# Delta-rule branch: decay columns of all heads made ahead of head 0, the rate moved into the exponent, pieces and queue positions changed

## What is computed

```python
g = jnp.cumsum(g, axis=-1)
decay = jnp.exp(jnp.where(incl, g[..., :, None] - g[..., None, :], -jnp.inf))
k_beta = k * beta[..., None]
a_mat = jnp.einsum("bhnid,bhnjd->bhnij", k_beta, k) * jnp.where(strict, decay, 0.0)
sol = lax.linalg.triangular_solve(eye + a_mat, rhs, left_side=True, lower=True, unit_diagonal=True)
qk = jnp.einsum("bhnid,bhnjd->bhnij", q, k) * decay
q_dec = q * jnp.exp(g)[..., None]
k_dec = k * jnp.exp(g_last - g)[..., None]
# scan over chunks
v_new = u_c - w_c @ s
o = qd_c @ s + qk_c @ v_new
s = s * jnp.exp(gl_c) + kd_c^T @ v_new
```

## Time and profile before

| | us |
|---|---|
| median of 3 runs | 3056.8 |
| lowest, highest | 3055.17, 3057.97 |
| profiled execution, its own time | 3061.32 |
| profiled execution, its span | 3059.6 |

### The profile page before, as it was taken

One profiled execution on the slowest core, in us unless ns is written; L12 is line 12 of the kernel. 1 busy time (PEld: TensorE's weight loads), 2 busy tenths in 40 slices (PEclk: granted clock), 3 DMA queues, 4 the chain that ended last, 5 costly groups with the idle time before them and its releaser, 6 DMA issues. The chain is left out here.

```text
span 3059.6 us, 38554 instructions
## 1 busy us (share of the span) xinstructions
PE 2888.3 (94%) x15219; PEld 2356.4 (77%) x15219; DVE 1299.4 (42%) x1953; ACT 1072.4 (35%) x1829; POOL 1206.5 (39%) x805
## 2 busy tenths in 40 slices
PE   6999999999999969578778999999999999999998
PEld 5878787877888846477667887878888888888887
DVE  5233233321479949666564353322233232232323
ACT  4241313243044539455544122332333333333232
POOL 2222122121123320423421433466666666766663
PEclk9999999999999979878798999999999999999999
DMA  4434233343545357210103546332322333332331
GB/s 114 165 132 140 80 102 102 100 132 94 184 148 176 120 189 249 80 44 31 73 31 126 179 141 208 105 100 93 102 91 91 103 96 124 97 97 91 114 110 58
DMA packets 239571, 352.78 MB, mean 115 GB/s; under 512 B 32928, under 2 KB 186272, under 8 KB 239392
## 3 DMA queue, kind: packets, MB, share of 16 engines
q1 hardware_dynamic: 239392, 350.32, 35.2%
HBM read 263.71 MB, written 96.36 MB: 118 GB/s over the span
## 5 line engine op out<-in xcount | busy, mean ns | idle before, releaser
L102 PE MATMUL pj_acc<-u_hi,pj_w_hi 128*128 128x512 f32 x1464 | 576.6, 394 | 10.6 <-DVE u_lo L823 10.6
L2763 DVE TENSOR_TENSOR x_tm<-m_ps,x_tm 128x512 f32<-128x512 f32 x384 | 265.0, 691 | 745.8 <-PE m_ps L104 745.8
L104 PE MATMUL pj_acc<-u_hi,pj_w_lo 128*128 128x512 f32 x1464 | 571.9, 391 | 0.0
L103 PE MATMUL pj_acc<-u_lo,pj_w_hi 128*128 128x512 f32 x1464 | 571.7, 391 | 0.0
L551 POOL TENSOR_TENSOR pj_w_lo<-pj_w_raw,pj_w_hi 128x1024 fp32r<-128x1024 f32 x61 | 159.2, 2610 | 722.0 <-ACT pj_w_hi L600 722.0
L2645 POOL TENSOR_TENSOR m_lo<-gate,held 128x1024 fp32r<-128x1024 f32 x96 | 237.8, 2500 | 270.0 <-ACT held L2562 270.0
L102 PEld LDWEIGHTS pj_acc<-u_hi,pj_w_hi 128*128 128x128 f32 x1464 | 275.9, 188 | 85.7 <-issue 18.2
L104 PEld LDWEIGHTS pj_acc<-u_hi,pj_w_lo 128*128 128x128 f32 x1464 | 276.1, 189 | 58.2
L103 PEld LDWEIGHTS pj_acc<-u_lo,pj_w_hi 128*128 128x128 f32 x1464 | 276.2, 189 | 56.2
L102 PE MATMUL m_ps<-held 128*128 128x512 f32 x768 | 299.7, 390 | 2.4 <-DVEq L2744 2.4
L102 PE MATMUL m_ps<-held,m_h_hi 128*128 128x512 f32 x768 | 299.5, 390 | 0.0
(11 more groups left out here) (308 smaller groups left out, 4939.8 us busy)
## 6 DMA issues: line engine op xcount, KB each, us to landing
gate<-in_w_mlp_dram SPq DMA_DIRECT2D x48, 1024.0 KB, 5.4
gate<-in_w_mlp_dram SPq DMA_DIRECT2D x96, 512.0 KB, 3.7
proj<-pj_stage SPq DMA_DIRECT2D x61, 768.0 KB, 3.4
pj_w_raw<-in_w_in_dram SPq DMA_DIRECT2D x61, 512.0 KB, 5.2
gate<-proj SPq DMA_DIRECT2D x24, 768.0 KB, 4.4
mo_w_raw<-in_w_out_dram SPq DMA_DIRECT2D x48, 256.0 KB, 2.9
rpb_bias<-pj_shut SPq DMA_DIRECT2D x48, 192.0 KB, 3.1
rpb_bias<-rpb_near SPq DMA_DIRECT2D x24, 384.0 KB
```

Of the source, the lines that this page charges most:

```text
L102: pe.matmul(out, w_hi, x_hi, start=first, stop=False)
L103: pe.matmul(out, w_hi, x_lo, start=False, stop=False)
L104: return pe.matmul(out, w_lo, x_hi, start=False, stop=last)
L2763: dve.tensor_tensor(xt, ps2[:, q % 4], xt, ALU.add).then_inc(added, 1)
```

## The change

- The columns of all 4 heads are made once: `gneg` (minus the cumulated decay), `gbeta` (decay plus the logarithm of beta, by ACT's Ln) at the head of attention, and `cx` in head 0's preparation. The chunks' last rows come from two matmuls of a broadcast column of the identity with `cols`; they stand in front of `gram(0, 0)` on PE and wait for two DVE copies, which stand behind DVE's wait for the norm weights' DMA. `decay_columns` and `columns` at k = 6 are gone.
- Beta enters the exponent, so `scores` is one instruction of 128x512.
- `decayed_queries` is 6 pieces of 128x512. The exponentials of `gq` move from k = 0 and 2 of the solve phase to steps 5 and 6 of the scan before (for head 0 into its preparation).
- ACT's `cut_blocks` moves ahead of the output copies of step 2, DVE's behind the state copies of step 2. Of the 16 placing copies into `un`, ACT now makes 4 (of `c1`, after the first transpose), DVE 12.
- The positions in the solve phase and in the scan move as the constants say. `out_lengths` is split into 3 pieces of 8 matmuls at k = 3, 4, 5. `out_gate` goes from k = 12 to k = 15, the sigmoid product (`ZGATE_IN`) from step 5 to step 6.

```diff
-def decay_columns(dve, c, cols, col, ncol, cx, gq):
...
 attention, DVE:
+            dve.tensor_scalar(gbeta[:], cols[:, :, 2:4], 1e-30, None, ALU.max).then_inc(d_rates, 1)
+            dve.tensor_scalar(gneg[:], cols[:, :, 0:2], -1.0, None, ALU.mult).then_inc(d_cols, 1)
...
                 if u == DCOL_AT:
-                    dve.wait_ge(dg_in, 32)
-                    dc = Chain(dve, d_chain, 0, 8)
-                    decay_columns(dve, dc, cols[:, 0], col2[:, 0], ncol2[:, 0], cx2[:, 0], gq[:, 0])
+                    dve.wait_ge(d_rates, 2)
+                    dve.tensor_tensor(gbeta[:], cols[:, :, 0:2], gbeta[:], ALU.add).then_inc(d_cols, 1)
 attention, ACT:
+            act.wait_ge(d_rates, 1)
+            act.activation(rates, rates, ACT.Ln).then_inc(d_rates, 1)
...
-SQUARES_AT, ROOT_AT, EG_AT, CEXP_AT = 1, 5, (0, 2), 10
-LENGTHS_AT, MEAN_AT, DIAG_AT, SPREAD_AT, NORM_AT, GATE_AT = 2, 3, 5, (7, 9, 11), (8, 10, 12), 12
-TURN_AT = (0, 3, 6, 9, 11, 13)
-TOKEN_AT = ((1, 2), (4, 5), (7, 8), (10, 11), (12, 13), (14, 15))
-COLUMNS_AT = 6
-INCL_AT = {8: 4, 11: 5, 13: 0, 15: 1}
+SUM_AT, SQUARES_AT, LENGTHS_AT, MEAN_AT, ROOT_AT, DIAG_AT = 0, 2, (3, 4, 5), 6, 8, 8
+SPREAD_AT, NORM_AT, GATE_AT = (10, 12, 14), (11, 13, 15), 15
+TURN_AT = (0, 2, 5, 8, 11, 13)
+TOKEN_AT = ((0, 1), (2, 3), (5, 6), (9, 10), (11, 12), (13, 14))
+INCL_AT = {9: 4, 12: 5, 15: 0}
...
-INCL_END = {1: 3, 3: 2}
+INCL_END = {1: 1, 3: 3, 4: 2}
-QK_IN = {0: (4, 5), 1: (0, 1), 4: (3, 2)}
-CUT_IN, WIDE_IN, ZTANH_IN, ZGATE_IN, SPREAD_IN = 2, 3, 4, 5, 7
+QK_IN = {0: (4, 5), 2: (0, 1), 5: (3, 2)}
+CUT_IN, WIDE_IN, ZTANH_IN, ZGATE_IN, SPREAD_IN = 2, 3, 4, 6, 7
+EG_IN = (5, 6)
...
 POOL:
-                    pool.tensor_tensor(gq[:, i % 2, d], gq[:, i % 2, d], y2[:, i % 2, 0], ALU.mult).then_inc(S["qd"], 1)
+                    for tb in range(NTB):
+                        r = slice(tb * TB, (tb + 1) * TB)
+                        pool.tensor_tensor(gq[:, i % 2, d, r], gq[:, i % 2, d, r], y2[:, i % 2, 0, r], ALU.mult).then_inc(S["qd"], 1)
...
 ACT, place:
+                for q in Q32:
+                    act.copy(by_direction(un, q, 0)[:, 0:NTB:2, :, q], compact(c1, q, 0)[:, 0:NTB:2]).then_inc(S["un0_d0"], 1)
...
 PE, ahead of gram(0, 0):
+            pe.wait_ge(S["ends"], 2)
+            for d in range(2):
+                last = pe.matmul(ps[:, 3, d, 0:HEADS * NT], work[:, d * P:(d + 1) * P], cols[:, :, d], start=True, stop=True)
+            last.then_inc(S["ends"], 1)
...
 DVE, scores and the head of its list:
-                for j in range(4):
-                    last = dve.scalar_tensor_tensor(am[:, n, j], ps[:, 4 + 2 * (GRAMS.index(tg) % 2), j],
-                                                    ncol2[:, i % 2, 2 + d, 4 * tg + j:4 * tg + j + 1], decays[:, j], ALU.mult, ALU.mult)
+                dve.scalar_tensor_tensor(am[:, n], ps[:, 4 + 2 * (GRAMS.index(tg) % 2)], -1.0, decays, ALU.mult,
+                                         ALU.mult).then_inc(S["am_done"], 1)
...
+            for d, row in ((0, P - 1), (1, 0)):
+                dve.tensor_copy(work[:, d * P:(d + 1) * P], ident[:, row:row + 1].to_broadcast([P, P])).then_inc(S["ends"], 1)
             dve.memset(ps[:, 0:2], 0.0).then_inc(S["blank"], 1)
```

More of the change, by code:

```diff
@@ L1281, in _ @@
                 if u == DEXP_AT:
-                    act.wait_ge(d_cols, 1)
-                    flat = cx2[:, 0].rearrange("p a t -> p (a t)")
-                    act.activation(flat, flat, ACT.Exp).then_inc(d_colexp, 1)
+                    act.wait_ge(d_cols, 2)
                 if DEXP_AT <= u < U:
@@ L1381, in deltanet @@
     with Space(nc, "dn") as s:
-        names = ("y_in0", "y_in1", "z_in", "g_in", "prm_in", "stored", "out_done", "chain",
-                 "kt_mm", "kt_ev", "cols_in", "cexp", "eg", "qd", "gram", "mask_s", "mask_i", "exp_s", "exp_i", "am_done", "qk_done",
-                 "cleared", "cut_a", "cut_d", "wide", "solve", "spread", "un0", "tn0_act", "tn0_pool",
+        names = ("y_in0", "y_in1", "z_in", "g_in", "prm_in", "stored", "out_done", "ends", "columns",
+                 "kt_mm", "kt_ev", "cexp", "eg", "qd", "gram", "mask_s", "mask_i", "exp_s", "exp_i", "am_done", "qk_done",
+                 "cleared", "cut_a", "cut_d", "wide", "solve", "spread", "un0_d0", "un0_d1", "un0_late", "tn0_act", "tn0_pool",
                  "s_mm", "s_ev", "u_mm", "u_ev", "t_mm", "t_ev", "ks", "r", "new_mm", "new_ev", "o_mm", "o_ev", "st_mm", "st_ev",
@@ L1654, in main @@
                         out_root(i - 1)
[L1655 to L1662, removed]
                     if k in INCL_AT and more:
@@ L1675, in main @@
                         strict_decays(i + 1, STRICT_MID[step])
+                    if more and step == CUT_IN:
+                        cut_blocks(i + 1)
                     for j, d, t in live_chains(step):
@@ L1693, in main @@
                     place(i + 1)
-            act.sem_inc(S["cexp"], 1)
             act.sem_inc(S["exp_s"], NG6)
             act.sem_inc(S["exp_i"], NG6)
+            act.wait_ge(S["columns"], 5)
+            flat_cx = cx[:].rearrange("p h a t -> p (h a t)")
+            act.activation(flat_cx, flat_cx, ACT.Exp).then_inc(S["cexp"], 1)
+            for d in range(2):
+                row_decays(0, d)
             cut_blocks(0)
@@ L1948, in prepare, with main @@
                     narrow(i)
-                    place(i, True)
-            def main(i, more, c, nxt):
-                if i:
-                    out_sum(i - 1)
+            def main(i, more):
                 for k in range(NS):
@@ L1968, in main @@
                     if i:
+                        if k == SUM_AT:
+                            out_sum(i - 1)
                         if k == MEAN_AT:
@@ L1976, in main @@
                             out_gate(i - 1)
-                    if k == COLUMNS_AT and more:
-                        columns(i + 1, nxt)
                 dve.sem_inc(S["s0"], 1)
@@ L1997, in main @@
                         if step:
[L1998 removed]
+                            dve.scalar_tensor_tensor(st[:, j], st[:, j], cx[:, i, EGL[d], t:t + 1], ps[:, j, 2], ALU.mult, ALU.add).then_inc(S["st_ev"], 1)
                         else:
                             dve.tensor_copy(st[:, j], ps[:, j, 2]).then_inc(S["st_ev"], 1)
+                    if more and step == CUT_IN:
+                        cut_blocks(i + 1)
                 if more:
[L2002 to L2004 removed]
+                    place(i + 1)
             dve.wait_ge(S["prm_in"], 16)
[L2006 removed]
+            for d, row in ((0, P - 1), (1, 0)):
+                dve.tensor_copy(work[:, d * P:(d + 1) * P], ident[:, row:row + 1].to_broadcast([P, P])).then_inc(S["ends"], 1)
             dve.memset(ps[:, 0:2], 0.0).then_inc(S["blank"], 1)
[L2008 to L2013 removed]
+            for step in range(STEPS):
+                prepare(0, step)
+                if step == 0:
+                    columns()
+                if step == CUT_IN:
+                    cut_blocks(0)
+                if step == WIDE_IN:
+                    rates()
+            place(0)
             for i in range(HEADS - 1):
[L2015 to L2016 removed]
+                main(i, True)
+            main(HEADS - 1, False)
             dve.wait_ge(S["gated"], HEADS)
```

134 lines of the change are left out of this document (60 added, 74 removed).

## The result

Before: 3056.8 us, the median of 9 runs (3054.7 to 3060.6). After: 3065.2 us, 9 runs (3061.4 to 3089.2). The ratio is 1.0037, with a 95% interval of 1.0020 to 1.0053: **8.4 us slower** by the medians (the ratio is not the quotient of the medians; by its interval it is 6 to 16 us). The forecast was 3056.0, no change, in a range of 3037 to 3068. So the time lies in the range, but the direction is wrong: "same" had 0.35, "slower" 0.22.

A forecast was written before the change was run, and what follows sets the result against it. Outside attention and DeltaNet PE was taken as practically full; within DeltaNet, engine-to-engine chains and a low clock bound it. Gains and losses summed to -0.7 us, giving 3056.1 us for the median, in a range of 3037 to 3068.

The forecast's parts named there:

- placing: Copies into un at each head's solve start: six DVE copies each wait for a POOL query piece, +14.7 us together.
- Rival A: DVE's copies pass POOL's instructions, so preparation is 4.7 and placing 14.7 us less: 3037 us, chance 0.2.
- Preparation: Head 0's preparation: two DVE copies ahead of gram wait for POOL's two memsets, +5.8 us.
- Attention: Unit 6 of attention: column instructions beside POOL's masks go, -4.7, softmax operations meet POOL instead, +1.7; net -3 us.
- Solve phases: Solve phases of all heads: columns, gq exponentials, turns, spreads and the placing's part behind the first u copy, -24.2 us.
- the turns: Solve phase: the last two turns of each head no longer wait for tokens of the u copy just before, -17.3 us.
- the gq exponentials: Two ACT exponentials of 1.48 us leave each solve phase for the scan: -1.5 each in heads 1 to 3, -4.5 us.
- The wait at k = 2: Solve phase, PE's second turn: PE stands still for 3.3 us until DVE's second token product.
- The tail: Solve phase's end into the scan: later gate delays the store, ACT waits for it at the scan's head, +11.2 us.
- Rival D: The store lands before ACT needs it and so hides: 3046 us, chance 0.05.
- B: Without the columns' stalls the clock stays high in solve phases, about 4 us in each of three heads: 3044, chance 0.14.
- C: The clock falls at PE's new wait at k = 2, products 4 to 5 us longer in heads 1 to 3: 3069, chance 0.23.

The follow-up runs named there:

- e13: Changed kernel with only POOL's masks for the next head put behind DVE's last placing copy, the six query pieces left beside the copies: 3043.8 us, ratio 0.9969 to before.
- e2: Changed kernel with POOL's query pieces and the masks after them waiting for DVE's last placing copy: 3037.6 us, ratio 0.9938 to the kernel before.
- the second profile: The kernel before, unchanged, profiled a second time: 3054.3 us, where its first profiled execution took 3061.3.
- e8: Changed kernel with the two identity-column copies in head 0's preparation made by ACT instead of DVE: one run, 3060.1 us.
- e3: Changed kernel with ACT's wait for the store moved from the scan's head to just ahead of the first output copy: 3065.7 us, ratio 1.0030 to before.
- e4: Changed kernel with POOL behind the placing and ACT's store wait ahead of the first output copy: 3029.4 us, ratio 0.9910 to the kernel before.
- e5: Changed kernel with 13 unused extra PE products in the placing's waits of each of heads 1 to 3: 3065.5 us, ratio 1.0033 to before.
- e9: Changed kernel with the turns at k 0, 3, 6, 9, 11, 13 and their token products moved: 3077.1 us, ratio 1.0077 to the kernel before.
- e10: Changed kernel with turns at k 0, 3, 6, 9, 11, 13 plus the extra PE products in the placing: 3063.2 us, ratio 1.0023 to before.

## Why the prediction was wrong

**The step that failed: placing.** "Each of the next six then waits for a piece, and the last is done at 1379.7": the mechanism was right, the count was not. The term stood in the sum at +14.7, of it +10.8 up to the first u copy, and the masks were in it with nothing. I followed POOL's six pieces and stopped there. Right behind them POOL's list has the six masks of the next head, which wait for nothing at that moment. So twelve copies waited instead of six, in three heads of four: +26 us up to the first u copy instead of +10.8. Head 3 has no masks and cost 3.0, close to the 2.7. e13 takes the masks away and gets close to the forecast's own number in every head (2.9 to 3.6); e2 takes all away and is 26 us faster by the fastest runs. Against the second profile attention, preparation and scans came out better than forecast by 3, 2 and 6 us and the solve phases worse by 5, which is why the whole is off by less than the placing.

A copy of 32x128 took 1.19 us here and 0.22 alone, about one POOL instruction for each copy. By the Trainium skill (SBUF — State Buffer, "Who interferes with whom"), when DVE is in a 2-port mode the engine that issues first has the shared ports for its whole instruction and the other waits it out. The 1.19 us agrees.

**Rival A**, that copies pass POOL, is out. The 0.17 us spoke for another kind of instruction.

**Preparation**: +3.4 to 3.5 instead of +5.8, mis-sized: the copies did wait (2.50 us), but for the rest of one memset, not for both. e8 shows that 4.0 hang on these copies, about half of it on POOL and half on the wait for the norm weights ahead of them.

**Attention**: -6.4 instead of -3 against the second profile, of which up to 0.8 may again be the scatter of the bias transfer. Before, the columns cost 6.0, of which 1.0 is left (one instruction of 1.03 us). The +1.7 that I added for later softmax operations beside POOL isn't seen in the sum.

**Solve phases**: forecast -24.2, measured -19.3 to -25.3. A part of it is PE's work that moved into the placing, and the clock differs between the profiles, so the agreement with the sum is in part luck. Single terms where they were tried: the turns -20.2 (forecast -17.3; the clock of head 3 is in it), the gq exponentials -3.6 by the windows (-4.5) and nothing visible in the run times. The wait at k = 2 was 2.2 us, not 3.3. The columns and the spreads were not tried alone.

**The tail**: right in its order (gate at 1413.25, store, ACT idle for 7.1 us), but +7.1 by the windows of e3 and +6.3 by those of e4 against e2, not +11.2; so the first step seems to have had more room. Rival D, that the store hides, is out (it was priced at 10, though the term in the sum is 11.2).

**Rivals B and C** asked the right question of the wrong place. In the traces at hand the clock falls during or behind standstills of PE of 2 us and more, as C said: in after's placing of head 1 (3.85 and 4.87 us) and at the head of its scan, and in e5 at k = 2 (2.46). B's solve phases at a high clock came with the mended placing (0.92 to 0.95 in e4). Neither could be planned: filling the waits of the placing moved the fall to the next standstill, and e2, with the placing as short as in e4, had 0.73 in head 2.

**The base.** I set the sum against a profiled execution that lay 4.5 above the median and said so, but read its stages as typical. The solve phases of heads 1 and 2 were 5.6 us longer in it than in the second profile (46.2 and 47.4 against 43.9 and 44.1), and attention 2.4. That is why the sum against the first trace comes out at +0.6 and hides the loss.

What stays open: why the same kernel takes 3061 in one execution and 3080 in the next. It goes with the mean clock; which standstill decides, and what ends a low stretch, the runs did not show. A run without the standstill at k = 2 in heads 1 and 2 was not made.

## What to carry to other kernels

When an engine's work is moved earlier, read on in its list: what follows the moved instructions moves too, and here it did nearly as much harm as they (13.7 and 17.8 us by the windows). A chain of small copies beside a chain of instructions on an engine that locks them out pays one whole instruction for each copy as long as both chains last. Put the long chain behind the short one with a wait; that one line was worth 26 us by the fastest runs. When an edit is meant to remove a standstill, check in the trace that it is gone: in e9 and e10 another engine's wait had taken its place. And where the clock is uneven, profile the kernel before twice, before a sum is set against its stages.

## What the runs showed of the hardware

PE's clock was not given back by work alone. In e5 it stayed at 1.2 GHz for 48 us in which PE was busy for 45.8. Behind the placing of head 1 in after's trace the granted clock was 0.50 from 1372 to 1382, 1.00 for the next 2 us, and then 0.50 again from 1386 to 1398, with PE busy throughout; from 1400 it was 1.00. The Trainium skill (TensorE: Matmul & The Clock Gate, "What's actually happening") says that activity releases the throttle; this stretch does not agree, or not with busy time as the profile counts it. The small transposes of PE (L1783) show the level at a glance: 0.27 us at 2.4 GHz, 0.42 to 0.47 at 1.2.

The cost goes both ways. In e2 and e13 six POOL instructions of 128x512 took 8.93 and 8.99 us, where the six pieces of e13 took 7.54. Five of the six took some 1.27 each as elsewhere, and one 2.80 and 2.83: in e13 this one stood beside DVE's `out_sum`, which reads 128x1536 from SBUF and took 1.75.
